# The weights of two input norms: loaded as rows and transposed on TensorE, in place of element-wise loads

## The chip, the cores and the metric

The kernel runs on 1 core of one Trainium2 chip. The metric is the device time of one execution in microseconds (us). Before the change it is 1379.03 us, the median of 3 runs (1378.55 to 1379.48).

## The reference, cut to what matters

The reference is one inference step of a hybrid decoder layer, for a prompt of 512 tokens and 8 sample tokens, model width 1024, all in float32. Two of its norms have a weight vector that is applied ahead of a projection:

```python
def rmsnorm(x, g):
    y = x32 * lax.rsqrt(jnp.mean(x32 * x32, axis=-1, keepdims=True) + EPS)
    return (y * g.astype(jnp.float32)).astype(x.dtype)
...
h  = rmsnorm(x, w['norm_mix_pre'])      # ahead of w_in
z  = h @ w_in                           # queries, keys and values, gates, S5 channels
...
x  = x + rmsnorm(merged @ w['w_out'], w['norm_mix_post'])
hm = rmsnorm(x, w['norm_mlp_pre'])      # ahead of w_mlp_up
```

`norm_mix_pre` and `norm_mlp_pre` are vectors of 1024 floats (4 KB). Beside attention there is a state-space branch (S5), whose complex decay rates, powers and lag matrices are computed from small parameter tables at the start of the kernel.

## The kernel before

**The layout.** Activations lie feature-major in `hT` (128 partitions x 8 feature tiles x 520 tokens). So a norm's weight of feature tile k is a column of 128 values, and `gT` (128 x 2 x 8) holds both vectors as such columns. In DRAM a vector is contiguous, and the load at lines 602 to 604 puts element k*128+p on partition p, column k: 1024 elements of 4 bytes for each vector.

**The first norm.** SyncE's queue (SP) issues in this order: the identity (line 597), four tiles of x (line 599), the sample rows (600), the rest of the constants (601), the two weight vectors (603), and then the stream of weight slabs (649 and after), with some small loads between the slabs. ScalarE computes each token tile's sum of squares and its root (`rms`, lines 864 and 857). VectorE runs `pre_norm` (from line 1178): for each of five token tiles a reciprocal (1198), a scaling of the tile (1201), and, one tile behind, `evac`: two products of a transposed half tile in PSUM with the weights in `gT` into `hT` (1187). TensorE transposes the scaled tiles (`norm_transposes`, each transpose is at line 1735) and then goes over to the projections (line 1758).

**The parameters ahead of it.** ACT's queue loads three small tables into `nat` (16 rows), TensorE transposes them into bank 0 of PSUM (lines 1769 to 1773), VectorE copies them to `par3` (1208), and then computes the angles of the S5 decay (1210 to 1217) before it starts `pre_norm`. ScalarE waits for `par3` (line 874) before its exponential at 875 and the `rms` loop behind it. Its sine and cosine work (881 and after) waits for `ang_ready`, which line 1217 gives. Behind `pre_norm` VectorE has a long chain of S5 tables (lines 1220 to 1290), from which GpSimd (from line 740) and ScalarE (line 907) take their start.

**The second norm.** `pre_norm(10, ...)` runs at about 939 us with column 1 of `gT`.

**What orders the work.** Each engine's program is written out by hand in program order, with semaphores between the engines. GpSimd's queue issues four loads of the S5 input matrices (line 734) at the start. The weight slabs go through three buffers, each refilled when `slab_used` says so.

Of the kernel before, what the change touches and what calls it, by code (L numbers as in the profile page):

```python
# [13 lines left out]
P = 128  # L14
D = 1024
KD = D // P
# [163 lines left out]
def build(nc, a):  # L180
    with ExitStack() as ctx:
        def sb(name, shape, dt=F32):
            return ctx.enter_context(nc.sbuf_tensor(name, shape, dt))

        def sem(name):
            return ctx.enter_context(nc.semaphore(name))
# [7 lines left out]
        QO = sb("QO", [P, 2 * KD * NT])  # L194
# [15 lines left out]
        def tiny(n):  # L210
            used[0] += n
            assert used[0] <= 1696
            return small[:, used[0] - n:used[0]]


        gT = tiny(2 * KD).rearrange("p (w k) -> p w k", w=2)
        par3 = tiny(3 * NST)
        are, aim, ldt = (par3[:, NST * k:NST * k + NST] for k in range(3))
        dt, mag, ang, ang2, sn, sh, cs, mag4 = (tiny(NST) for _ in range(8))
# [20 lines left out]
        PS = ctx.enter_context(nc.psum_tensor("PS", [P, 8, 512], F32))  # L240
# [2 lines left out]
        consts_in = sem("consts_in")  # L243
        masks_in = sem("masks_in")
        x_in = [sem(f"x_in_{t}") for t in range(TT + 1)]
        g_in = [sem(f"g_in_{w}") for w in range(2)]
        pages_in = sem("pages_in")
        rows_ready = sem("rows_ready")
        perm_ready = sem("perm_ready")
# [135 lines left out]
        STP = QO[0:NST, 6720:6976].rearrange("p (c r) -> p c r", r=2)  # L385
        nat = QO[0:NST, 3120:3504].rearrange("p (k c) -> p k c", k=3)
        ldt2 = QO[0:NST, 3504:3506]
        bld = R[:, 0:512].rearrange("p (r i c) -> p r i c", r=2, i=NST)
        bwk = R[:, 512:1536].rearrange("p (r i c) -> p r i c", r=4, i=NST)
        xtm = KVU[:, 0:5 * D].rearrange("p (t d) -> p t d", d=D)  # L390
# [205 lines left out]
        def _(sp):  # L596
# [3 lines left out]
            sp.dma_start(xtm[0:NB, TT, :], a["x_sample"].rearrange("b o d -> (b o) d")).then_inc(x_in[TT], 16)  # L600
            sp.dma_start(consts[:, P:CO_N], a["consts"][:, P:CO_N]).then_inc(masks_in, 16)
            for w, name in enumerate(("norm_mix_pre", "norm_mlp_pre")):
                sp.dma_start(gT[:, w, :], a[name].rearrange("(k p) -> p k", p=P),
                             allow_slow_non_contiguous=True).then_inc(g_in[w], 16)

            def small_loads():

# [13 lines left out]
            def compression_weights():  # L621
                sp.wait_ge(ends_full, 4)

                for k, kv in enumerate("kv"):
# [8 lines left out]
                    for half in range(2):  # L633
                        sp.dma_start(w2[64 * k:64 * k + 64, 64 * half:64 * half + 64],
                                     a[f"cmp_w2_{kv}"]).then_inc(w1_in, 16)

            for n, (kind, arg, count, _) in enumerate(PLAN):
                if (kind, arg) == ("q", (0,)):
                    compression_weights()
# [7 lines left out]
                if kind == "win":  # L647
                    c0, w = arg
# [72 lines left out]
        def _(pool):  # L721
# [67 lines left out]
            for n, (kind, arg, _, count) in enumerate(PLAN):  # L789
                if count == 0:  # L790
                    continue
                pool.wait_ge(slab_used, n - NS + 1)
                if kind == "cmp":
                    b, half = arg
                    for c in range(2):
                        pool.indirect_dma_start(  # L796
                            slab(n)[:, 2048 * c:2048 * c + 2048], None, cmp_rows, bass.IndirectOffsetOnAxis(
                                ap=row_cmp[:, 4 * b + 2 * half + c:4 * b + 2 * half + c + 1], axis=0)).then_inc(rows_in[n % NS], 16)
                    continue
                dst = slab(n).rearrange("p (x c) -> p x c", x=16)  # L800
                for x in range(1, 16, 2):
                    at = slab_page(arg, x, kind == "kpage")
                    pool.indirect_dma_start(dst[:, x, :], None, slc_rows, bass.IndirectOffsetOnAxis(  # L803
                        ap=row_kv[:, at:at + 1], axis=0)).then_inc(rows_in[n % NS], 16)
# [42 lines left out]
        def _(act):  # L847
# [65 lines left out]
            for u, unit in enumerate(UNITS):  # L913
# [46 lines left out]
                elif kind == "trg":  # L960
                    nc.scalar.activation(gs8[0:NB, :], pr[0:NB, 1, 0:3 * NH], ACT.Copy)
                    ins = nc.scalar.activation(gtm[:, :, :],
                                               pr[:, 0, 0:TT * 3 * NH].rearrange("p (t c) -> p t c", t=TT), ACT.Copy)
                elif kind == "ft":
                    _, ri, q = unit
                    ins = nc.scalar.activation(ET[:, ri, 8 * q:8 * q + 8, :],
                                               pr.rearrange("p h (i c) -> p (h i) c", i=4), ACT.Copy)
# [200 lines left out]
        def _(dve):  # L1168
            n_ch = [0]

            def link(ins):
                n_ch[0] += 1
                ins.then_inc(dve_ch, 1)
                dve.wait_ge(dve_ch, n_ch[0])

            V = nc.vector
            V.memset(epsb, EPS).then_inc(eps_ready, 1)
            def pre_norm(first, src, dst, gains, roots, make=None):

                def evac(t):  # L1180
                    if t == 0:
                        dve.wait_ge(g_in[first // 10], 16)
                    for half in range(2):
                        v = first + 2 * t + half
                        w = ROWS[t]
                        dve.wait_ge(xnt_full, v + 1)
                        V.tensor_tensor(hT[:, 4 * half:4 * half + 4, P * t:P * t + w],  # L1187
                                        PS[:, 4 + v % 4, 0:4 * w].rearrange("p (k c) -> p k c", k=4),
                                        gains[:, 4 * half:4 * half + 4].unsqueeze(2).to_broadcast([P, 4, w]),
                                        ALU.mult).then_inc(xnt_free, 1)  # L1190

                if make:
                    make(0)
                for t, r in enumerate(ROWS):
                    if make and t + 1 < len(ROWS):
                        make(t + 1)
                    dve.wait_ge(root_ready, roots + t + 1)
                    link(V.reciprocal(rstd[0:r, t:t + 1], ssq[0:r, t:t + 1]))
                    if t >= 2:
                        dve.wait_ge(xnt_full, first + 2 * (t - 1))  # L1200
                    V.tensor_scalar(dst[0:r, t % 2, :], src[0:r, t, :], rstd[0:r, t:t + 1], None,
                                    ALU.mult).then_inc(xn_ready, 1)
                    if t:
                        evac(t - 1)
                evac(4)

            dve.wait_ge(par_full, 1)
            V.tensor_copy(par3, PS[:, 0, 0:3 * NST]).then_inc(par_ready, 1)
            dve.wait_ge(ldt_ready, 1)
            V.tensor_tensor(mag, are, dt, ALU.mult)  # L1210
            link(V.tensor_tensor(ang, aim, dt, ALU.mult))
# [324 lines left out]
            for n in range(NTK + 2):  # L1536
                if n < NTK:
                    t, p, h, r, nx = TASKS[n]
                    dve.wait_ge(as_full, n + 1)
                    k, bank = 4 * (n % 2), 2 * (n % 2)  # L1540
# [7 lines left out]
                if 1 <= n <= NTK:  # L1548
                    m = n - 1
                    dve.wait_ge(as_exp, m + 1)  # L1550
                    k, nx = 4 * (m % 2), TASKS[m][4]
# [7 lines left out]
                if n >= 2:  # L1559
                    m = n - 2  # L1560
                    t = TASKS[m][0]
# [95 lines left out]
            for w, (kind, c, x) in enumerate(SU):  # L1657
# [35 lines left out]
                if kind == "up":  # L1693
                    f = F[:, c % 2, 2 * x:2 * x + 2, :]
# [36 lines left out]
        def _(pe):  # L1731
            M = nc.tensor.matmul

            def tp(out, in_, rows=P):
                return nc.tensor.transpose(out, in_, ident[0:rows, 0:rows])  # L1735

            def norm_transposes(first, src):
                for v0, (t, half) in enumerate(NORM_UNITS):
                    v = first + v0
                    r = ROWS[t]  # L1740
                    pe.wait_ge(xn_ready, first // 2 + t + 1)
                    if v >= 4:
                        pe.wait_ge(xnt_free, v - 3)
                    for k in range(4):
                        ins = tp(PS[:, 4 + v % 4, r * k:r * k + r],
                                 src[0:r, t % 2, P * (4 * half + k):P * (4 * half + k) + P], r)
                    ins.then_inc(xnt_full, 1)
# [23 lines left out]
            for k in range(3):  # L1771
                ins = tp(PS[:, 0, NST * k:NST * k + NST], nat[:, k, :], NST)
            ins.then_inc(par_full, 1)
            norm_transposes(0, xn)
            pe.wait_ge(xnt_free, 10)

# [5 lines left out]
            def projection(u, unit):  # L1782
# [3 lines left out]
                if kind == "gemm":  # L1786
                    _, key, m, w, to = unit
                    n = SLAB[key]
                    wait_slab(pe, n)
                    width = 512 if w == P else w  # L1790
                    S = slab(n)[:, 0:KD * width].rearrange("p (k c) -> p k c", c=width)
                    ins = gemm(u, [S[:, k, P * m:P * m + w] for k in range(KD)], [hT[:, k, :] for k in range(KD)], w)
                    ins.then_inc(pair_full, 1)
                    if last_of[n] == u:
                        pe.wait_ge(pair_full, u + 1)
                        pe.sem_inc(slab_used, 1)  # L1796
                    return
# [158 lines left out]
            for r in range(len(KR) + 1):  # L1956
# [9 lines left out]
                if r in R_CS:  # L1966

                    t = R_CS.index(r)
# [266 lines left out]
```

## Time and profile before

| | before |
|---|---|
| median of 3 runs | 1379.03 us (1378.55 to 1379.48) |
| profiled execution, own time | 1379.02 us |
| its span | 1377.1 us |
| TensorE busy | 1262.2 us, 92% of the span |
| VectorE / ScalarE / GpSimd busy | 786.5 / 331.9 / 355.3 us |
| mean granted TensorE clock | 0.978 of full |

The profile is of one execution. The span goes from its first to its last instruction, and what lies around it (start and end of the program) is 1.9 us here. Shares of busy time are averages over stages with different limits: for a change at the start of the kernel the first 100 us are read in order of time.

### The profile page before, as it was taken

What the parts mean: (1) busy time and instruction counts of PE and PEld (TensorE: products, weight loads), DVE (VectorE), ACT (ScalarE), POOL (GpSimd) and SP (SyncE); (2) the same over time, 40 slices, a digit from 0 to 9 for tenths busy, and PEclk for the clock granted to TensorE, in tenths of its full rate; (3) what the DMA queues carried; (4) which work ended last, traced back from release to release, by engine and by line L of the source; (5) the groups of instructions that cost most, each with busy time, mean ns of one, the idle gap of its engine ahead of it and who ended that gap; (6) DMA issues with size and microseconds to landing.
All of it is one profiled execution on the core that took longest, in us unless ns stands there. A gap on an engine that the chain in (4) does not pass through costs nothing.

```text
span 1377.1 us, 19377 instructions
## 1 busy us (share of the span) xinstructions
PE 1262.2 (92%) x7099; PEld 1021.7 (74%) x7099; DVE 786.5 (57%) x1319; ACT 331.9 (24%) x889; POOL 355.3 (26%) x422
## 2 busy tenths in 40 slices
PE   6989999999978778889999999995999999999996
PEld 5878878887855545555678888784888888888885
DVE  6788001288833467767765545756565465467445
ACT  3375210100025465554411111023000000000012
POOL 4920000122357322222211111110111112413542
PEclk9999999999989999999999999996999999999998
DMA  9011461477657734433553323412113122132101
GB/s 286 3 67 30 101 146 62 164 271 265 255 164 221 261 110 118 147 104 118 164 236 112 96 57 110 151 62 77 62 61 123 61 77 108 61 111 74 62 0 63
DMA packets 123902, 165.88 MB, mean 120 GB/s; under 512 B 38496, under 2 KB 92304, under 8 KB 119456
## 3 DMA queue, kind: packets, MB, share of 16 engines
q1 hardware_dynamic: 105488, 104.73, 24.3%
q0 software_dynamic: 8080, 50.58, 10.3%
q10 hardware_dynamic: 10240, 9.33, 2.1%
q8 instruction: 57, 0.93, 0.3%
q14 instruction: 37, 0.30, 0.1%
HBM read 159.14 MB, written 13.84 MB: 126 GB/s over the span
## 4 chain that ended last, share of the span: by engine, by line
PE 77%; DVE 10%; ACT 5%; issue 4%; POOL 3%; DMA 1%; SPq 0%; DVEq 0%; PEldq 0%; ACTq 0%
PE PS L2136 44%; PE PS L1758 12%; PE PS L1893 9%; PE PS L1735 4%; POOL stream L803 3%; ACT R L1084 2%; DVE small L1547 2%; PE PS L1990 2%; PE PS L2022 2%; PE PS L2072 1%; DVE PS L1545 1%; DMA small<-in_norm_mix_pre 1%; ACT R L1093 1%; PE PS L1859 1%; DVE hT L1187 1%
## 5 line engine op out<-in xcount | busy, mean ns | idle before, releaser
L1758 PE MATMUL PS<-hT,stream 128*128 128x260 f32 (+1 forms) x800 | 182.8, 388 | 2.6 <-PE PS L1758 0.6
L1758 PEld LDWEIGHTS PS<-hT,stream 128*128 128x128 f32 (+1 forms) x800 | 150.9, 191 | 30.4 <-issue 1.4
L2136 PE MATMUL PS<-R,stream 128*128 128x260 f32 x720 | 168.9, 383 | 2.4 <-PE PS L2136 2.4
L2136 PEld LDWEIGHTS PS<-R,stream 128*128 128x128 f32 x720 | 135.9, 190 | 25.6 <-issue 5.5
L1381 DVE STREAM_TRANSPOSE R<-stream 128x2048 f32<-128x2048 f32 (+1 forms) x34 | 74.6, 2226 | 125.5 <-DMA stream<-out_kv_cmp_prompt 71.7
L2136 PE MATMUL PS<-R 128*128 128x260 f32 x576 | 132.7, 387 | 3.3 <-DVE R L1710 2.1
L2136 PEld LDWEIGHTS PS<-R 128*128 128x128 f32 x576 | 110.7, 193 | 21.5 <-DVE R L1710 2.5
L2136 PE MATMUL PS<-R,QO 128*128 128x260 f32 x544 | 123.6, 383 | 1.4 <-DVE QO L1591 1.4
L1893 PE MATMUL PS<-R 128*128 128x256 f32 (+1 forms) x544 | 120.1, 377 | 3.2 <-PE PS L1893 2.3
L2136 PEld LDWEIGHTS PS<-R,QO 128*128 128x128 f32 x544 | 103.4, 190 | 17.4 <-DVE QO L1591 1.8
L1665 DVE TENSOR_TENSOR R<-PS,R 128x260 f32<-128x260 f32 x100 | 42.6, 426 | 128.2 <-PE PS L2136 127.4
L1893 PEld LDWEIGHTS PS<-R 128*128 128x128 f32 x544 | 99.1, 190 | 21.4 <-issue 8.8
L2136 PE MATMUL PS<-hT,stream 128*128 128x260 f32 x384 | 94.8, 391 | 3.7 <-PE PS L2136 3.0
L1665 DVE TENSOR_TENSOR KVU<-PS,KVU 128x260 f32<-128x260 f32 x92 | 39.3, 427 | 100.8 <-PE PS L2136 90.3
L796 POOL DMA_INDIRECT stream<-in_cache_kv_cmp,row_cmp x32 | 30.2, 943 | 255.0 <-PEq L1796 179.8
L1735 PEld LDWEIGHTS PS<-consts,R 128*128 128x128 f32 (+2 forms) x441 | 48.6, 143 | 57.5 <-ACT R L1093 42.9
L1735 PE MATMUL PS<-consts,R 128*128 128x128 f32 (+2 forms) x441 | 63.1, 285 | 27.1 <-ACT R L1093 22.6
L1137 ACT ACTIVATE R<-PS 128x260 f32<-128x260 f32 x56 | 21.5, 386 | 272.2 <-PE PS L2136 272.2
L2136 PEld LDWEIGHTS PS<-hT,stream 128*128 128x128 f32 x384 | 73.2, 193 | 18.6 <-issue 6.8
L1084 ACT ACTIVATE R<-PS,small 128x128 f32<-128x128 f32 (+3 forms) x128 | 66.0, 524 | 82.4 <-DVE small L1547 64.1
L581 POOL TENSOR_SCALAR R<-R,small 128x128 f32<-128x128 f32 (+3 forms) x64 | 48.2, 756 | 133.2 <-DVE small L1552 133.2
L803 POOL DMA_INDIRECT stream<-in_cache_kv_slc,row_kv x64 | 61.4, 960 | 37.0 <-issue 18.9
(401 smaller groups left out, 1940.7 us busy)
## 6 DMA issues: line engine op xcount, KB each, us to landing
stream<-in_cache_kv_slc SPq DMA_DIRECT2D x192, 128.0 KB
stream<-in_w_mlp_up SPq DMA_DIRECT2D x8, 2048.0 KB
stream<-in_w_mlp_down SPq DMA_DIRECT2D x8, 2048.0 KB
stream<-in_w_in SPq DMA_DIRECT2D x4, 2048.0 KB
stream<-in_state_kv_win SPq DMA_DIRECT2D x16, 512.0 KB
stream<-in_w_in SPq DMA_DIRECT2D x8, 1024.0 KB
out_kv_win_sample<-in_state_kv_win POOLq DMA_DIRECT2D x1, 8176.0 KB, 42.9
stream<-in_w_in SPq DMA_DIRECT2D x16, 256.0 KB
```

The source lines that it names most:

```text
L581: return eng.tensor_scalar(S, S, ainv[:, k:k + 1], gtm[:, t, col:col + 1], ALU.mult, ALU.mult)
L796: pool.indirect_dma_start(slab(n)[:, 2048 * c:2048 * c + 2048], None, cmp_rows, bass.IndirectOffsetOnAxis(ap=row_cmp[:, 4 * b + 2 * half + ...
L803: pool.indirect_dma_start(dst[:, x, :], None, slc_rows, bass.IndirectOffsetOnAxis(ap=row_kv[:, at:at + 1], axis=0)).then_inc(rows_in[n % N ...
L1084: ins = nc.scalar.activation(PP[:, n % 2, j, c0:c0 + P * (t + 1)], score_block(n, j, c0), ACT.Exp, bias=amx[:, k:k + 1], accum_out=asm[:, ...
L1381: V.transpose(ROWST[:, w % 3, 0:256 * ns].rearrange("p (s x) -> p s x", x=256), slab(s)[:, 0:512 * ns].rearrange("p (s k x) -> p k s x", k ...
L1547: V.reduce_max(amx[:, k:k + 2 * nx], S[:, :, 0:P * (t + 1)], AX, negate=True).then_inc(as_max, 1)
L1665: V.tensor_tensor(to, product_of(w, i), other, ALU.add).then_inc(pr_added, 1)
L1735: return nc.tensor.transpose(out, in_, ident[0:rows, 0:rows])
L1758: ins = M(pair(u)[0:w, hf, 0:HALF], lhs[k], rhs[k][:, HALF * hf:HALF * hf + HALF], start=(k == 0), stop=(k == n - 1))
L1893: ins = M(out, w1c[:, kind, x, :], rhs, start=(x == 0), stop=(x == 7))
L1990: ins = M(score_block(n, j, c0), qT[64 * j:64 * j + 64, 4 * p + h + x, P * t:P * t + P], kT[64 * j:64 * j + 64, 2 * r + p, 0:P * (t + 1)], ...
L2136: ins = M(product_of(w, i), lhs[:, k, :], rhs[:, k, :], start=(k == 0), stop=(k == nk - 1))
```

## The change

Each weight vector is loaded as 8 rows of 128 floats (512 bytes) into `gnat`, 16 rows in all, in an otherwise unused part of `QO`. Both loads count on one semaphore. TensorE transposes `gnat` once into bank 1 of PSUM, between the transposes of the S5 tables and those of the norm. VectorE copies the 128 x 16 result to `gT`, between the copy of `par3` and the angles. The wait of the first product on the loaded vector is gone.

```diff
         gT = tiny(2 * KD).rearrange("p (w k) -> p w k", w=2)
+        gflat = gT.rearrange("p w k -> p (w k)")
...
-        g_in = [sem(f"g_in_{w}") for w in range(2)]
+        gains_in = sem("gains_in")
+        gains_full = sem("gains_full")
+        gains_ready = sem("gains_ready")
...
+        gnat = QO[0:2 * KD, 3520:3648]
...
             for w, name in enumerate(("norm_mix_pre", "norm_mlp_pre")):
-                sp.dma_start(gT[:, w, :], a[name].rearrange("(k p) -> p k", p=P),
-                             allow_slow_non_contiguous=True).then_inc(g_in[w], 16)
+                sp.dma_start(gnat[KD * w:KD * w + KD, :], a[name].rearrange("(k p) -> k p", p=P)).then_inc(gains_in, 16)
...
                 def evac(t):
-                    if t == 0:
-                        dve.wait_ge(g_in[first // 10], 16)
...
             V.tensor_copy(par3, PS[:, 0, 0:3 * NST]).then_inc(par_ready, 1)
+            dve.wait_ge(gains_full, 1)
+            V.tensor_copy(gflat, PS[:, 1, 0:2 * KD]).then_inc(gains_ready, 1)
+            dve.wait_ge(gains_ready, 1)
             dve.wait_ge(ldt_ready, 1)
...
             ins.then_inc(par_full, 1)
+            pe.wait_ge(gains_in, 32)
+            tp(PS[:, 1, 0:2 * KD], gnat, 2 * KD).then_inc(gains_full, 1)
             norm_transposes(0, xn)
```

## Rows read from the trace of the kernel before

**Rows 1.** The page: the chain that ended last, shares of the span by engine.

```profile
PE 77%; DVE 10%; ACT 5%; issue 4%; POOL 3%; DMA 1%; SPq 0%; DVEq 0%; PEldq 0%; ACTq 0%
```

**Rows 2.** The chain in order of time, 0 to 120 us: start, length, what.

```profile
2.60 0.43 SPq L599
...
4.09 10.80 DMA small<-in_norm_mix_pre
...
61.42 1.11 DVE QO L1290
62.61 0.63 ACT R L907
...
69.53 1.09 PE PS L1735 x8
```

**Rows 3.** Timeline, 0 to 24 us: start, length, engine, line, what, [idle before].

```profile
3.69 0.35 SPq L601 DMA_DIRECT2D consts<-in_consts  x1
...
4.58 2.08 SPq L603 DMA_DIRECT2D small<-in_norm_mlp_pre  x1
...
5.80 0.39 PEld L1735 LDWEIGHTS PS<-consts,QO 16*128 16x128 f32 x3 [5.80 <-issue]
...
6.34 0.21 DVE L1208 COPY small<-PS 128x48 f32<-128x48 f32 x1 [5.48 <-PE PS L1735]
...
6.83 0.17 DVE L1210 TENSOR_TENSOR small<-small 128x16 f32<-128x16 f32 x1 [0.28 <-ACT small L875]
6.90 1.63 POOL L734 DMA_DIRECT2D R<-in_s_b_im  x2
...
9.48 0.17 DVE L1198 RECIPROCAL small<-small 128x1 f32<-128x1 f32 x1 [0.94 <-ACT small L857]
9.68 0.75 DVE L1201 TENSOR_SCALAR QO<-KVU,small 128x1024 f32<-128x1024 f32 x1
...
10.49 3.67 PE L1735 MATMUL PS<-consts,QO 128*128 128x128 f32 x16 [4.18 <-DVE QO L1201]
...
14.92 1.29 DVE L1187 TENSOR_TENSOR hT<-PS,small 128x512 f32<-128x512 f32 x2 [3.11 <-DMA small<-in_norm_mix_pre]
14.93 1.28 ACT L881 ACT_TABLE_LOAD   x1
...
21.08 1.47 DVE L1187 TENSOR_TENSOR hT<-PS,small 128x512 f32<-128x512 f32 x4
```

**Rows 4.** DMA issues of 0 to 15 us: count, KB each, median us to landing.

```profile
consts<-in_consts SPq DMA_DIRECT2D x1, 303.0 KB, 7.7
...
R<-in_s_b_im POOLq DMA_DIRECT2D x2, 64.0 KB, 6.8
...
small<-in_norm_mix_pre SPq DMA_DIRECT2D x1, 4.0 KB, 10.8
small<-in_norm_mlp_pre SPq DMA_DIRECT2D x1, 4.0 KB, 10.5
```

**Rows 5.** Timeline of TensorE, 22 to 104 us.

```profile
22.60 16.01 PE L1758 MATMUL PS<-hT,stream 128*128 128x260 f32 x64 [0.38 <-DVE hT L1187]
...
82.19 3.97 PE L1859 MATMUL PS<-QO,R 128*128 128x136 f32 x16 [4.25 <-issue]
85.95 7.97 PE L1758 MATMUL PS<-hT,stream 128*128 128x260 f32 x32
...
94.31 2.02 PE L1859 MATMUL PS<-QO,R 128*128 128x136 f32 x16
96.16 7.18 PE L1758 MATMUL PS<-hT,stream 128*128 128x260 f32 x32
```

**Rows 6.** The tensor x_prompt in 0 to 16 us, its four loads.

```profile
DMA to landing us min/median/max: 3.7/5.5/7.7
```

**Rows 7.** Stretches: stretch, length, busy of the engines, granted clock, DMA share, GB/s.

```profile
10.00:12.00 2.00, 1.51 (x7) 1.51 (x8) 1.36 (x3) 1.94 (x6) 0.00 (x0) 1.00 1.14 113
```

**Rows 8.** One stretch of TensorE alone: stretch, length, busy, granted clock, DMA share, GB/s.

```profile
82.20:86.10 3.90, 3.90 (x17) 0.50 0.02 6
```

## The prediction

> **What bounds the kernel now.** First the page's chain of work that ended last [rows 1]: 77% of the span is TensorE, and 1% is a DMA. Then the same chain in order of time [rows 2]: that 1% is one piece, the load of the first weight vector, from its issue at 4.09 for 10.80 us. Behind it the chain runs over VectorE without a break of more than a microsecond, through the norm and the S5 tables, the last of them at 61.42, then ScalarE at 62.61, and reaches TensorE at 69.53. So the end of the first norm on VectorE sets the time of all that follows, and a shift of it is passed on. Then the timeline of the first 24 us [rows 3], to see what the load holds up: VectorE stands idle for 3.11 us before its first product at 14.92. This is the only wait on either vector that the trace has; the second vector, used at about 939 us, is never waited for. The two loads were issued at 4.09 and 4.58 and landed 10.8 and 10.5 us later [rows 4], at 14.89 and 15.08.
>
> So at most about 3.1 us (0.22% of the time) is on the table. The question is only what replaces the wait.
>
> **What the change removes.** The 3.11 us of idling, if the vectors come early. 2048 elements of 4 bytes on the DMA engines; SP's second issue, 2.08 us (at 4.58), becomes like that of the constants, 0.35 (at 3.69) [rows 3], so the first weight slabs are issued 1.7 us earlier, and their data comes earlier by what the elements took. I put this at nothing: the first projection at 22.60 was released by VectorE's product, not by a slab [rows 5]. The cover is the norm itself. The same goes for the other small loads behind the slabs.
>
> **What it adds and moves.** One transpose and one copy, which are small, and one wait, which is not: TensorE, and then VectorE, wait for both vectors before anything of the norm. In the kernel before, the angles (6.83 to 8.54), the reciprocal and scaling of tiles 0 and 1, and the transposes of both (16 in 3.67 us, 0.229 each) ran while the vectors were on their way; only the products waited [rows 3]. Now the angles, the scaling and the transposes all stand behind the wait. Call G the moment at which both vectors have landed. From G to the end of the first pair of products:
>
> - transpose until VectorE's copy starts: three such transposes took 5.80 to 6.34, 0.54 us [rows 3]. One lies between a third of it, 0.18, and 0.54; I take 0.30, as the start and the end are paid once;
> - the copy: 0.21 for 48 columns (row at 6.34), with the hand-over to itself 0.23;
> - the angles: 6.83 to 8.54 (the reciprocal at 9.48 had been idle for 0.94), with the step to the next 1.75;
> - reciprocal and scaling of tile 0: 0.20 (9.48 to 9.68) and 0.75;
> - to TensorE 0.06 (10.43 to 10.49); eight transposes at 0.229, 1.84; the second half's product behind them 0.05 and 0.64 (half of 1.29). The first half's product and the scaling of tile 1 lie beside these transposes.
>
> The sum is 0.30 + 0.23 + 1.75 + 0.95 + 0.06 + 1.84 + 0.69 = 5.82. Before, this pair ended at 14.92 + 1.29 = 16.21. What follows it keeps its order and its rate: VectorE needs about 2.05 us for each tile (products 1.29, scaling 0.75), TensorE 1.84 for its transposes, so VectorE stays the bound up to 21.08 + 1.47 = 22.55 in the trace before. The norm thus shifts by (G + 5.82) - 16.21 = G - 10.39. **The break-even is a landing at 10.4 us.** The three branches that the shift touches: ScalarE's wait for the angles is hidden as long as they end (G + 0.53 + 1.72) before 14.93, where it takes up that work [rows 3], so for G below 12.7, and even a later one has cover up to VectorE's use of the sines after 22.5; GpSimd starts from a product of VectorE's chain and shifts with it; `rms` on ScalarE is released by `par3`, whose copy stays ahead of the new wait. The second norm loses a wait that was never one.
>
> **When do the vectors land?** The trace has no 512-byte rows of this kind, so G is bounded by neighbours on the same queue. Below: the last tile of x, which stands ahead, was issued at 2.60 and landed 7.7 us later [rows 2, 6], at 10.3. Between: the constants, just ahead of the vectors, issued at 3.69, landed at 11.39 [rows 3, 4]. Above: 14.9, as the elements did. The queue is nearest to the constants: the rows stand right behind them, with 8 KB to move, and two loads of 4 KB that follow one another landed 0.2 apart (14.89 and 15.08) in the trace. I take 11.39 + 2 x 0.2 = **11.8**. That gives 11.8 - 10.4 = **+1.4 us**. The sum is made against the profiled execution, 1379.02, which stands at the median of the runs (1379.03): 1379.02 + 1.4 = **1380.4**. What a measurement of this kernel can tell from no change is about 0.2%, 2.8 us; the forecast is inside it, on the slow side.
>
> **The rivals.**
>
> *Early vectors.* Eight rows may use fewer DMA engines than the 128 rows of the constants, and pass on engines that are done sooner, between the last tile of x (10.3) and 11.2. For it: the constants' landing counts the slowest engine. Time: at G = 10.6, 1379.2; at 10.3 it is 1378.9. The Trainium skill ("DMA: Bandwidth & Descriptors", Why a DMA increments its semaphore by 16 and not by 1) states that a load is split over the largest number of engines, up to 16, that divides its slowest dimension, which makes 8 for 8 rows and 16 for the constants; no row of this trace shows the engines one by one. A gain of more than 2.8 us would need G = 7.6, when x itself was not there, so this rival ends at no change.
>
> *Late vectors, slower than before.* GpSimd's loads of the S5 matrices, 64 KB each, share the DMA engines: the last is issued at about 7.7 (half of 1.63 behind 6.90) and lands 6.8 us later [rows 3, 4], at 14.5, and in 10 to 12 us the engines move 113 GB/s at a share above 1, so they are busy with small pieces [rows 7]. If the rows or their completion wait for that traffic, G is 13.1 to 14.9. It decides from 13.2 on (more than +2.8): at 14.5, +4.1, 1383.1. Against it: the constants passed the same traffic and landed at 11.39. The Trainium skill ("DMA: Bandwidth & Descriptors", Queues, rings and completion order) states that the increment of a DMA's semaphore lands only after every earlier write of that DMA engine, across its queues; no run here shows it yet, and the constants' landing speaks for little of it.
>
> *The shift is not passed on.* If another engine had slack behind the norm that the chain doesn't show, the time stays 1379.0. Against it: the chain is VectorE's from the norm to 61.42.
>
> *The granted clock falls elsewhere.* In 82.20 to 86.10 the granted clock was 0.50, 1.2 GHz, behind 4.25 us in which TensorE did nothing [rows 5, 8]: 16 products took 3.97 there and 2.02 at 94.31; the next 32 took 7.97, and 7.18 at 96.16. One such dip costs 1.95 + 0.79 = 2.7 us. One less gives 1380.4 - 2.7 = 1377.7; one more, 1383.1. Nothing around that idle time changes but its start.
>
> *The change doesn't do what it says* is only possible in its aim: the element loads do go.
>
> **How the numbers follow.** Forecast (G from 11.2 to 13.1, +0.8 to +2.7) 0.57; early vectors 0.14; not passed on 0.09; late vectors 0.10; a dip less 0.05, a dip more 0.05. Faster by over 0.2% (below 1376.3) comes only from a dip less along with early vectors, or from something that I don't see: 0.05. Slower by over 0.2% (above 1381.8): late vectors, a dip more: 0.15. Within: 0.80. The range leaves out most of the late case and the dips: from G = 10.3 with 0.4 of scatter, 1378.5, to G = 13.4 and scatter, 1382.5.
>
> **What would show it.** Right: the wait on the first vector at VectorE's first product is gone, and VectorE has a wait for TensorE of some 5 us at the copy of 16 columns, ending near 12.1; the first reciprocal near 14.1 (before 9.48), the first product near 16, the first projection near 24.0 (before 22.60), the first chain piece of ScalarE near 64.0 (before 62.61). The slabs land earlier and nobody notices. Wrong: the copy before 10.7 (early) or after 13.4 (late); a first projection shifted by one amount and ScalarE's piece at 62.61 by another (slack); a stretch of clock 0.50 that has come or gone; a first projection released by a slab.

## The result, and the profile after

The changed kernel takes 1381.45 us (median of 20 runs), the kernel before 1378.76 us in the same comparison: ratio 1.0019 with a 95% interval of 1.0012 to 1.0026. That is 2.6 us slower, 0.19%, just inside the 0.2% taken as the bound of no change, and clear of zero. Ratios and means here and below leave out three single slow runs: 1987 us of the changed kernel here, 7247 us of the kernel before beside the e experiments, and 3330 us of e2. The forecast was 1380.4 us, +1.4. The profiled execution of the changed kernel is the slowest of its other 19 runs (1384.2 us, with a span of 1382.4), 5.2 us above the profiled one of before, so its sum has to be read with care.

The chain of the changed kernel in order of time, 0 to 120 us (start, length, what):

```profile
4.11 0.37 SPq L607
...
4.52 6.51 DMA QO<-in_norm_mlp_pre
11.03 0.04 issue
11.07 0.30 PE PS L1739
...
22.91 15.99 PE PS L1762 x64
...
69.14 1.08 PE PS L1739 x8
```

The load is still a piece of the chain [rows 2], but now it holds TensorE, ahead of one transpose, and no longer VectorE ahead of its first product. Behind the norm the chain also takes another way: over TensorE's own projections from 22.91 on, where in the kernel before it went over VectorE's S5 tables and ScalarE. Both ways start at the end of the norm, so a later norm delays both. The timeline of the same 24 us, against [rows 3] (start, length, engine, line, what, count, idle before):

```profile
6.37 0.21 DVE L1209 COPY small<-PS 128x48 f32<-128x48 f32 x1 [5.50 <-PE PS L1739]
...
11.07 0.28 PE L1739 MATMUL PS<-consts,QO 16*128 16x16 f32 x1 [4.74 <-DMA QO<-in_norm_mlp_pre]
11.39 0.17 DVE L1211 COPY small<-PS 128x16 f32<-128x16 f32 x1 [4.81 <-PE PS L1739]
...
12.82 0.16 DVE L1199 RECIPROCAL small<-small 128x1 f32<-128x1 f32 x1
13.01 0.75 DVE L1202 TENSOR_SCALAR QO<-KVU,small 128x1024 f32<-128x1024 f32 x1
...
14.96 1.28 ACT L884 ACT_TABLE_LOAD   x1
14.97 0.69 DVE L1188 TENSOR_TENSOR hT<-PS,small 128x512 f32<-128x512 f32 x1 [0.35 <-PE PS L1739]
...
15.82 0.69 DVE L1188 TENSOR_TENSOR hT<-PS,small 128x512 f32<-128x512 f32 x1 [0.16 <-PE PS L1739]
...
21.39 1.47 DVE L1188 TENSOR_TENSOR hT<-PS,small 128x512 f32<-128x512 f32 x4
...
22.91 5.46 PE L1762 MATMUL PS<-hT,stream 128*128 128x260 f32 x16 [0.73 <-DVE hT L1188]
```

The wait of 3.11 us is gone. In its place VectorE idles 4.81 us ahead of the copy of 16 columns, and the first reciprocal has moved from 9.48 to 12.82: angles, scaling and transposes stand behind the wait, as the prediction had it. ScalarE takes up the sine tables at 14.96, where it did so at 14.93, so that branch kept its cover. The norm's last products end at 21.39 + 1.47 = 22.86, against 22.55. In this pair of profiles the whole head of the kernel costs 0.3 us.

So the heads of the two profiles don't explain 2.6 us, and far less their own 5.2. Most of the 5.2 lies where the granted clock was 0.50 (1.2 GHz) in one and full in the other. TensorE in some stretches of the changed kernel (stretch, length, busy, granted clock, DMA share, GB/s):

```profile
529.50:532.60 3.10, 3.10 (x35) 0.50 0.43 125
884.60:887.70 3.10, 3.10 (x8) 0.50 0.98 350
```

and in the same places of the kernel before:

```profile
524.00:532.00 8.00, 6.08 (x68) 1.00 0.43 117
882.00:888.00 6.00, 6.00 (x29) 1.00 0.98 378
```

Held side by side, the 32 products of line 2078 took 3.50 us at the first place, against 1.92 for the same products (line 2072) in the kernel before, and 24 products of line 2142 took 7.22 us at the second, against 5.53 (line 2136): the distance of the two kernels grows by 1.6 and by 1.7 us. Two explanations were open: scatter of the clock, which the change has no part in, or a change that brings more of these stretches.

### The profile page after: what moved, and what is told of

Same layout as the page of the kernel before. It is cut to its first block, busy times and chain, and to the rows that moved or that the text cites. A ratio compares the mean times of both kernels' runs of the same rounds, so it can differ in the third digit from the quotient of the medians.

```text
span 1382.4 us, 19379 instructions
## 1 busy us (share of the span) xinstructions
PE 1265.7 (92%) x7100; PEld 1022.4 (74%) x7100; DVE 786.9 (57%) x1320; ACT 332.5 (24%) x889; POOL 355.4 (26%) x422
## 4 chain that ended last, share of the span: by engine, by line
PE 79%; DVE 7%; ACT 5%; issue 4%; POOL 3%; DMA 1%; SPq 0%; DVEq 0%; PEldq 0%; ACTq 0%
PE PS L2142 44%; PE PS L1762 14%; PE PS L1899 9%; PE PS L1739 4%; POOL stream L806 3%; ACT R L1087 2%; DVE small L1551 2%; PE PS L1996 2%; PE PS L2028 2%; PE PS L2078 1%; DVE PS L1549 1%; ACT R L1096 1%; PE PS L1826 1%; PE PS L1865 1%; PE PS L1956 1%
## 5 line engine op out<-in xcount | busy, mean ns | idle before, releaser
L1140 ACT ACTIVATE R<-PS 128x260 f32<-128x260 f32 x56 | 21.5, 386 | 273.8 <-PE PS L2142 273.8
## 6 DMA issues: line engine op xcount, KB each, us to landing
stream<-in_w_in SPq DMA_DIRECT2D x4, 2048.0 KB, 10.8
```

## The experiments

The experiments with the letter e ran together on one chip, then those with f on a second, then those with g on a third. The kernel before takes 1412.4 us beside e, 1411.3 beside f and 1380.1 beside g. Each ratio is against the kernel before on the same chip. The absolute times in the expectations of e are those of the first comparison. "Head theory" means that the time follows the end of the first norm, "clock theory" that the change brings more stretches of the lower clock. The end of the norm is the end of the row of four products of line 1187 (1188 or 1192 in the edited kernels).

**e1_again and f2_changed: the changed kernel twice more.** No edit.

> The changed kernel once more, for its clock in a second profile. Head theory (the time moves one for one with the end of the first norm, which came 0.3 us later in the first profile): 1379.1, and the first profile's other 5 us were scatter. Clock theory (the change makes more stretches of 1.2 GHz likely, each worth 0.7 to 1.7 us): 1381.4 again, mean granted clock near 0.973 in every run against 0.975 or more of the kernel before, and the shift of the first norm again only 0.3 us.

> The changed kernel a third time, beside f1 on the same chip. Head theory: +0.3 to +1 us against f1. If something beyond the head is at work: +2.5 to +4 us again (first comparison 2.6, second 3.7 between means), to be found behind 390 us in the trace.

Ratios 1.0028 (1.0010 to 1.0046) and 1.0029 (1.0017 to 1.0042), +4.0 and +4.1 us. So the loss is real; whether it is larger than in the first comparison is open, as the intervals overlap. The mean granted clock over the runs was 0.9607 in e1 and 0.9611 in the kernel before beside it, 0.9617 and 0.9627 in f2. If TensorE had worked all the time, a mean lower by 0.0004 would cost 0.0004 x 1412 = 0.6 us, and one lower by 0.0010 would cost 1.4 (an estimate): not 4 us in either. The first part of e1's expectation, scatter alone, falls, and the clock theory gets little support. f2's expectation of +0.3 to +1 missed as well. What it put against that, a loss behind 390 us, isn't needed: f2's norm ends at 24.25, 3.7 us behind f1's (below). The rows landed at 10.5 in e1 and at 12.4 in f2 (a few rows of f2's timeline):

```profile
12.46 0.28 PE L1739 MATMUL PS<-consts,QO 16*128 16x16 f32 x1 [5.73 <-DMA QO<-in_norm_mlp_pre]
...
22.78 1.47 DVE L1188 TENSOR_TENSOR hT<-PS,small 128x512 f32<-128x512 f32 x4
```

**f1_before_itself and g1_before_twice: the kernel before against itself.** No edit.

> The kernel before, unchanged, timed as if it were a change: what the comparison gives when nothing differs, and the profile of this chip that the others are held against. Head theory: ratio 1.000 within 0.1%. If the ratio of two sets of runs of one kernel is off by 0.1 to 0.2% as well, most of the +2.6 us is scatter.

> The kernel before once more, for a second profile of it beside the others of this call. Landing theory: what the first comparison of profiles hid is that the element loads mostly land earlier than 14.9 (12.9 in f1, 13.0 in f4, 12.6 in e3), so that VectorE hardly waits in the kernel before; expected here: first vector at 12.6 to 13.1, wait below 0.7 us, first product near 12.9, last products end near 20.6. Rival (the late landing of the first profile is the usual one): 14.9.

Ratios 1.0003 (0.9989 to 1.0018) and 1.0002 (0.9992 to 1.0012): the comparison finds nothing where there is nothing. The profiles show why the pair above had only 0.3 us in its heads. DMA issues of g1, 0 to 15 us (count, KB, us to landing), and then its timeline:

```profile
small<-in_norm_mix_pre SPq DMA_DIRECT2D x1, 4.0 KB, 8.7
small<-in_norm_mlp_pre SPq DMA_DIRECT2D x1, 4.0 KB, 9.5
```

```profile
12.79 1.29 DVE L1187 TENSOR_TENSOR hT<-PS,small 128x512 f32<-128x512 f32 x2 [0.20 <-DMA small<-in_norm_mix_pre]
...
18.95 1.47 DVE L1187 TENSOR_TENSOR hT<-PS,small 128x512 f32<-128x512 f32 x4
...
20.47 5.75 PE L1758 MATMUL PS<-hT,stream 128*128 128x260 f32 x25 [0.73 <-DVE hT L1187]
```

And f1's:

```profile
12.92 1.29 DVE L1187 TENSOR_TENSOR hT<-PS,small 128x512 f32<-128x512 f32 x2 [0.67 <-PE PS L1735]
...
19.09 1.47 DVE L1187 TENSOR_TENSOR hT<-PS,small 128x512 f32<-128x512 f32 x4
```

The first vector landed at 12.8 in g1 (4.10 + 8.7) and at 12.9 in f1 (4.09 + 8.8). VectorE waited for it 0.20 us in g1; its 0.67 us in f1 is a wait for TensorE's transposes. The norm ended at 20.42 and 20.56, 2.1 and 2.0 us earlier than in the profile on which the prediction rests. In these two profiles the kernel before hardly has the wait that the change removes (all six are counted at g2).

**e2_rows_late and g3_rows_late_again: the rows, with the wait in another place.** The two lines of TensorE stand behind the transposes of tile 0, those of VectorE ahead of the first product.

```diff
-            dve.wait_ge(gains_full, 1)
-            V.tensor_copy(gflat, PS[:, 1, 0:2 * KD]).then_inc(gains_ready, 1)
-            dve.wait_ge(gains_ready, 1)
...
                 def evac(t):
+                    if first == 0 and t == 0:
+                        dve.wait_ge(gains_full, 1)
+                        V.tensor_copy(gflat, PS[:, 1, 0:2 * KD]).then_inc(gains_ready, 1)
+                        dve.wait_ge(gains_ready, 1)
...
-            pe.wait_ge(gains_in, 32)
-            tp(PS[:, 1, 0:2 * KD], gnat, 2 * KD).then_inc(gains_full, 1)
...
+                    if v == 2:
+                        pe.wait_ge(gains_in, 32)
+                        tp(PS[:, 1, 0:2 * KD], gnat, 2 * KD).then_inc(gains_full, 1)
```

> Rows as in the change, but the transpose stands behind the first tile's transposes on TensorE and the copy just ahead of the first product on VectorE: the angles, the scaling and the transposes no longer wait. Both theories: vectors landed at 11.0, first product near 12.9 in place of 14.92, the first projection near 20.6 (before 22.60). Head theory: 1379.0 - 2.0 = 1377.0. Clock theory: the same gain less what more stretches of 1.2 GHz take; if it is the early idle time of TensorE that brings them, this one has as little of it as the kernel before and also gives 1377.0; if it is anything else in the new loads, about 1379.

> e2 again (same row loads, wait only ahead of the first product). Landing theory: the wait's place is the whole loss; the rows land at 10.5 to 13.4, so the first product comes at 12.9 to 14.0 and the time is that of the kernel before within 1 us, 3 to 4 us below the changed kernel (which had +3.7 and +4 in the two calls). Rival (the row loads or the added instructions cost something elsewhere): 1.002 or more.

Ratios 0.9997 (0.9977 to 1.0017) and 1.0006 (0.9996 to 1.0015): not to be told from the kernel before, and e2 is 3.9 us below e1 in the mean. Loads, transpose and copy are those of the change; only the place of the wait differs. From g3's timeline:

```profile
13.66 0.17 DVE L1186 COPY small<-PS 128x16 f32<-128x16 f32 x1 [0.91 <-PE PS L1740]
...
13.87 1.29 DVE L1192 TENSOR_TENSOR hT<-PS,small 128x512 f32<-128x512 f32 x2
...
20.03 1.47 DVE L1192 TENSOR_TENSOR hT<-PS,small 128x512 f32<-128x512 f32 x4
```

In e2 the rows landed late, at 13.4 us. In g3 the profile shows no wait for them: the 8 transposes of tile 0 and that of `gnat` stand in the chain as one piece (11.44 to 13.64), and VectorE's copy came behind them. With the work ahead of the wait done, the norm ends at 21.5 (21.7 in e2). That is still 1.1 us behind g1 and f1, a loss that the two intervals neither show nor exclude. e2's expectation of a gain of 2 us missed, as it was made against the late landing of the first profile.

**e3_elements_barrier: the element loads, with the change's wait.**

```diff
             V.tensor_copy(par3, PS[:, 0, 0:3 * NST]).then_inc(par_ready, 1)
+            dve.wait_ge(g_in[0], 16)
+            dve.wait_ge(g_in[1], 16)
...
             ins.then_inc(par_full, 1)
+            pe.wait_ge(g_in[0], 16)
+            pe.wait_ge(g_in[1], 16)
             norm_transposes(0, xn)
```

> The element-wise loads of before with the change's wait: TensorE and VectorE wait for both vectors ahead of the angles and the transposes. Both landed at 15.1 before; from there 4.9 us to the end of the first pair of products (what the changed kernel showed, less its transpose and copy): 20.0 against 16.2, +3.8. Head theory: 1382.6. Clock theory: TensorE is idle for 4 us longer still, so more on top: 1384 or above, mean clock 0.973 or less.

Ratio 1.0026 (1.0007 to 1.0045), +3.7 us, in the mean over its runs +4.0. The +3.8 of the expectation was met, but partly by luck: it was counted from a pair that ends at 16.2, and with f1's 14.2 more was due. The norm ended at 24.19 + 1.47 = 25.66, 5.1 us behind f1's. The mean clock was 0.9627, above that of the kernel before: the clock theory's 0.973 was a figure of the first chip, but also the direction that it asks for is not there. This clock may hide a part of the 5.1: among the 34 runs of the kernel before beside e, a mean clock higher by 0.001 went with a time shorter by about 0.8 us (0.7 beside f, 0.4 beside g; estimates by a straight line through the runs), so 0.0016 with about 1.3 us. Against the changed kernel (+4.0) the loads hardly differ in time: rows in place of elements bring the landing of the later vector forward (14.3 here, 10.5 to 12.4 there), and pay for a transpose and a copy.

**e4_filled: TensorE kept busy during the wait.**

```diff
+            for k in range(24):
+                tp(PS[:, 2, P * (k % 4):P * (k % 4) + P], ident)
             pe.wait_ge(gains_in, 32)
```

> The changed kernel with 24 transposes of the identity into an unused bank of PSUM while TensorE waits for the rows (6.3 to about 10 us). The end of the first norm stays where the change has it (22.9). Head theory: same time as the changed kernel. Clock theory, if idle time of TensorE in the head brings the additional stretches of 1.2 GHz: back to 1379, mean clock 0.975 or more; if something else does, 1381.4.

Ratio 1.0019 (1.0001 to 1.0037), +2.7 us, mean clock 0.9606, in the mean 1.2 us below e1. Its timeline of TensorE:

```profile
6.72 5.38 PE L1739 MATMUL PS<-consts 128*128 128x128 f32 x24
12.04 0.26 PE L1739 MATMUL PS<-consts,QO 16*128 16x16 f32 x1
```

Filling the idle time gives back at most a part of the time and nothing of the clock (0.9607 in e1). Together with the mean clocks of e1 and f2 this speaks against idle time of TensorE in the head as the cause of the loss. It doesn't exclude a gain of 1 to 3 us against e1, for two reasons: the runs of either scatter by 2.3 us (standard deviation, 12 runs each), and the 24 transposes ran until 12.1, not to about 10, so that the transpose of `gnat` may have waited for them and not for the rows. The norm ended at 23.1, 0.7 behind e1's.

**f4_delay and g2_delay_again: is a shift of the norm passed on?**

```diff
                     if t:
                         evac(t - 1)
+                    if t == 1 and first == 0:
+                        for _ in range(4):
+                            link(V.tensor_scalar(QO[:, 5000:6024], xtm[:, 0, :], 1.0, None, ALU.mult))
```

> The kernel before with four extra scalings of a tile (0.77 us each) on VectorE between the products of tile 0 and tile 1 of the first norm: nothing else differs, loads and waits are those of before. The first norm ends 3.1 us later. Head theory: +3.1 us. If the time is absorbed behind the norm: 0. If any shift of the head brings more stretches of 1.2 GHz: more than +4.

> f4 again, since its 6 runs gave +7.6 where its profile showed a norm 3.0 us later. Head theory: +3.1 us against the kernel before (ratio 1.0022). Rival (a shift of the head costs more than itself): +5 us or more once again.

g2's timeline of VectorE shows the edit:

```profile
14.75 1.29 DVE L1187 TENSOR_TENSOR hT<-PS,small 128x512 f32<-128x512 f32 x2 [2.00 <-DMA small<-in_norm_mix_pre]
15.96 2.87 DVE L1207 TENSOR_SCALAR QO<-KVU 128x1024 f32<-128x1024 f32 x4
...
19.72 1.28 DVE L1187 TENSOR_TENSOR hT<-PS,small 128x512 f32<-128x512 f32 x2
```

From the products of tile 0 to those of tile 1 it takes 4.97 us in place of 2.06: a delay of 2.9. g2: ratio 1.0022 (1.0011 to 1.0033), +3.0 us. It is passed on, one for one within the interval (+1.5 to +4.6). f4, of only 6 runs, gave 1.0054 (1.0037 to 1.0072), +7.6, more than twice the delay, while its profiled run was only 3.5 us above the mean of the runs of the kernel before beside it. Its mean clock was 0.9598 against 0.9627, which by the estimate at e3 goes with about 2 us; g2 doesn't repeat the +7.6, and the rest of it is open. g2 also shows the wait of 2.00 us on element loads again (landed at 14.8). So of six profiles with element loads, the first vector landed at 12.6 to 13.0 in four (e3, f1, f4, g1) and at 14.8 to 14.9 in two (the first profile and g2).

**f3_rows_first: the rows ahead of x.**

```diff
             sp.dma_start(consts[:, 0:P], a["consts"][:, 0:P]).then_inc(consts_in, 16)
+            for w, name in enumerate(("norm_mix_pre", "norm_mlp_pre")):
+                sp.dma_start(gnat[KD * w:KD * w + KD, :], a[name].rearrange("(k p) -> k p", p=P)).then_inc(gains_in, 16)
...
-            for w, name in enumerate(("norm_mix_pre", "norm_mlp_pre")):
-                sp.dma_start(gnat[KD * w:KD * w + KD, :], a[name].rearrange("(k p) -> k p", p=P)).then_inc(gains_in, 16)
```

> The changed kernel with the two row loads issued right behind the identity, ahead of x. The rows then land before 6 us, the wait costs nothing, angles and transposes run as early as in the kernel before, and the first product comes at about 11.8 in place of 14.92: the first norm ends 3 us earlier than before. Head theory: 3.0 us below f1 and 3.3 to 4 below f2. If the later stages take the gain back (transfers that start at times of their own): same as f1.

Ratio 1.0004 (0.9992 to 1.0015): back at the kernel before, 3.9 us in the mean below f2, and not 3.0 below f1 as the head theory had it. Its timeline:

```profile
4.58 0.21 DVE L1209 COPY small<-PS 128x48 f32<-128x48 f32 x1 [3.71 <-PE PS L1739]
4.71 0.17 DVE L1211 COPY small<-PS 128x16 f32<-128x16 f32 x1
...
17.56 1.47 DVE L1188 TENSOR_TENSOR hT<-PS,small 128x512 f32<-128x512 f32 x4
...
20.38 5.93 PE L1762 MATMUL PS<-hT,stream 128*128 128x260 f32 x14 [2.03 <-DMA stream<-in_w_in]
```

The wait costs nothing, the norm ends at 19.0, 1.5 us before f1's, and now the first projection is held by the weight slab for 2.03 us and starts at 20.38, where f1's starts at 20.61. The cover named in the prediction for the slabs, the norm itself, is gone: the slab is what is late next. That the slab alone takes the gain back isn't shown: f3's mean clock was 0.9602 against 0.9627, which by the estimate at e3 goes with about 1.7 us.

**g4_rows_first_masks_late: f3, with the large table of constants behind two slabs.**

```diff
-            sp.dma_start(consts[:, P:CO_N], a["consts"][:, P:CO_N]).then_inc(masks_in, 16)
...
                     if n == 1:
                         small_loads()
+                        sp.dma_start(consts[:, P:CO_N], a["consts"][:, P:CO_N]).then_inc(masks_in, 16)
```

> f3 (rows ahead of x) with the 303 KB of other constants moved behind the first two weight slabs. f3's norm ended at 19.0, but its projection waited 2.0 us more for the first slab. Slab theory: the slab lands 0.8 us earlier, so the first projection starts near 19.6, 1.0 us before the kernel before; time 1 to 2 us below it. Rival (the S5 chain or the clock sets the time anyway): no change against f3, 1.000.

1376.63 us against 1380.08, ratio 0.9977 (0.9968 to 0.9986): 3.2 us faster than the kernel before, more than the 1 to 2 us expected.

```profile
10.88 1.47 DVE L1188 TENSOR_TENSOR hT<-PS,small 128x512 f32<-128x512 f32 x2
...
17.22 1.47 DVE L1188 TENSOR_TENSOR hT<-PS,small 128x512 f32<-128x512 f32 x4
...
19.04 7.18 PE L1762 MATMUL PS<-hT,stream 128*128 128x260 f32 x24 [1.03 <-DMA stream<-in_w_in]
```

The first projection starts at 19.04, 1.4 us before g1's, and the wait on the slab is down to 1.03. The norm ends at 18.69, 1.7 us before g1's. The time gained more than either. That two of the six profiles with element loads have the later landing may be a part of it, and the mean clock another (0.9735 against 0.9725, about 0.4 us by the estimate at e3); the rest stays open.

## Why the prediction was right or wrong

The time lay inside the range and on the side that was forecast, slower. The size was off: +1.4 us was put, +2.6 measured in the first comparison and +4.0 and +4.1 in the next two. That the number came out inside the range is in part luck, as two errors pull against each other. With the kernel before as f1 shows it, the sum lacks 2.0 us (16.21 against 14.21); the landing of the first profile after takes 0.8 back (11.03 against 11.8) and the way from there 0.3: 1.4 + 2.0 - 0.8 - 0.3 = +2.3.

- **Right: what replaces the wait.** That angles, scaling and transposes stand behind the new wait is the loss, all of it or nearly so. e2 and g3, which differ from the changed kernel in the place of the wait alone, measure -0.4 and +0.8 us against the kernel before, with intervals that hold zero and reach up to +2.4 and +2.1.
- **Right: the way from the landing to the first products.** 5.82 us by the sum; in the first profile after, from the landing at 11.03 to 15.82 + 0.69 = 16.51, 5.48. The angles took 1.2 (11.60 to 12.82) where 1.75 was put: two of their seven instructions took 0.40 and 0.36 us in the kernel before (at 7.34 and 8.19) and 0.17 and 0.18 in the changed one. The eight transposes took 1.98 (13.82 to 15.80) where 1.84 was put.
- **Nearly right: the landing.** 11.8 was put, from the constants' landing and two steps of 0.2. Measured 11.03, 10.5 and 12.4 in the three profiles of the changed kernel, in each case 0.4 to 0.7 us behind the constants (in the first, 3.71 + 6.6 = 10.3, and 0.7 later the rows). The order of the queue held. The rival of an early landing on half of the DMA engines got no sign of its own, as the rows stayed behind the constants. For the late rival the rule of the Trainium skill ("DMA: Bandwidth & Descriptors", Queues, rings and completion order), that a semaphore's increment waits for the earlier writes of its engine across queues, would allow a landing as late as GpSimd's loads. The last two of these were issued from 6.91 on and took 7.5 us in the profile after, so they landed at about 14.4 or later, the rows at 11.03: the trace shows no such delay here. It is no test of the rule either, as GpSimd's loads were issued from 5.08 on and the rows at 4.11 and 4.52.
- **Wrong: the base of the sum.** "Before, this pair ended at 14.92 + 1.29 = 16.21", and with it "the break-even is a landing at 10.4 us". The 14.92 comes from a landing of the elements at 14.89 that one profile showed and that the prediction took for the kernel's. Four of six profiles have 12.6 to 13.0. Against those the pair ends at 14.21 (12.92 + 1.29 in f1), and with the measured 5.48 the break-even is a landing at 8.7 us, which no profile with the rows behind the constants reaches. The mis-sized term is thus the wait removed: 3.11 us by the one profile, 2.00 in g2, and at most 0.7 in f1, f4 and g1. The norm ends at 22.55, 20.56 and 20.42 in the three profiles of the kernel before and at 22.86, 22.36 and 24.25 in those of the changed one: 2.0 us apart in the mean, of the 2.6 to 4.1 measured. By the second 16 products of line 1859 (1865 after), which start at 94.31, 91.99 and 90.42 before and at 95.56, 94.19 and 96.12 after, the means are 3.1 apart. By these profiles the whole loss is there by 95 us, but they are three for each kernel and lie up to 4 us apart, so how it divides is not shown.
- **Right: a shift of the norm is passed on.** g2: 2.9 us of delay, 3.0 of time. The sign that was asked for is there too: in the profile after, the first projection moved from 22.60 to 22.91 and ScalarE's first piece from 62.61 to 62.94, by the same 0.3. (The places named, 24.0 and 64.0, were missed by 1.1: 0.8 for the earlier landing, 0.3 for the shorter way.) The rival with slack falls for a delay; for an earlier norm f3 shows the limit, the weight slab.
- **Right in kind: the clock.** Stretches of 0.50 come and go between executions: by the mean clocks of the two profiles, 0.978 and 0.972, the changed kernel's had some 17 us more of them (an estimate: (0.028 x 1382 - 0.022 x 1377) / 0.5). That explains most of the profiled run's 5.2 us. For the median's 2.6 it can't be said, as of the kernel before the first comparison has the clock of the profiled run only; over the runs of e1 the mean clock is nearly the same for both kernels.
- **Right: slabs and other loads early, at no gain,** as long as the norm is later. f3 shows what they cost when it is not.

## What to carry to other kernels

A wait that shows up in one profile on a small load behind megabytes of others may be a matter of that execution: look at the landing in several profiles before you put a number on its removal. When a load is made cheaper and gets a wait of its own, put the wait where the data is used and not where it is convenient to convert it; here that place alone was worth 3 to 4 us (e2 against e1, g3 against f2). Try a small load that much depends on at the head of its queue, and then look at what is late next (here a weight slab behind a table of constants that VectorE first reads at 82.25 us, line 1319, in the kernel before).

## What the runs showed of the hardware that had not been expected

- The first vector as 1024 elements of 4 bytes, loaded behind 2.4 MB on the same queue, landed 8.4 to 8.8 us after its issue in four profiles and 10.6 to 10.8 in two; nothing between. The second took 9.5 to 10.0 us in the same four and 10.5 to 10.6 in the same two.
- The same kernel takes 1379 to 1380 us in the first comparison and beside g, and 1411 to 1412 beside e and f, on other chips. The difference arises in one stage, the end of the compression and the first key pages: in g1 it runs from 373 to 444 us (71 us), in f1 from 376 to 483 (107 us); the rest differs by a few us. Why is open.
- The rows give the granted clock as 1.00 already in the stretch from 10 to 12 us [rows 7], but 16 transposes of 128 x 128 took 3.67 us from 10.49 on [rows 3], 0.229 each. In the profile after, the first norm's later ones took (timeline of TensorE)

```profile
19.49 1.09 PE L1739 MATMUL PS<-consts,QO 128*128 128x128 f32 x8 [0.96 <-DVE QO L1202]
```

0.136 each, and in the kernel before, with a granted clock of 0.50 beside them (timeline, and the stretch around it),

```profile
55.83 3.65 PE L1735 MATMUL PS<-consts,R 128*128 128x128 f32 x16
```

```profile
53.60:60.20 6.60, 6.60 (x31) 0.50 0.01 2
```

again 0.228. By these durations the clock was at its lower level, 1.2 GHz, in the first transposes, although the rows don't say so.
